# A hybrid decoder layer on one core: two score levels copied by ScalarE, the next head's work on other slots, and four weight pieces requested at once at the start

## The chip, the core and the metric

The kernel runs on 1 core of one Trainium2 chip. The metric is the device time of one execution in microseconds (us), the median of several runs. The core has five engines that run their own instruction lists in order and meet at semaphores: TensorE (PE in the profile, matmul; PEld is its weight load), VectorE (DVE), ScalarE (ACT), GpSimd (POOL) and SyncE (SP), which here only starts DMA transfers.

## What is computed

One layer of 512 tokens and 2048 channels, in float32:

```
h    = rmsnorm(x, norm_w)
proj = h @ w_in      # 2048 x 7184: gla q,k,v,gate,lowrank, hgrn q,f,i,gate
o_a  = 4 heads of chunked gated linear attention (dk 128, dv 256) on gla q, k, v, decay
o_b  = 8 heads of the same (dk 128, dv 128) on hgrn q, 1-f, i, log f
mixed = concat(head_rmsnorm(o_a) * silu(gate_a), head_rmsnorm(o_b) * silu(gate_b))
out  = rmsnorm(x + mixed @ w_out, final_norm_w)
```

Attention of a head: with b the running sum of the log decays, score(i, j) = sum over d of q_i k_j exp(b_i - b_j) for j <= i, output = scores @ v plus the decayed state of the chunks before.

## The kernel before

**Weights.** Every weight group is 2048 rows by 512 columns and comes in 8 pieces of 256 rows (512 KB). SyncE loads a piece into one of two `raw` slots; ScalarE rounds it to the high part `w_hi` (L847, helper `split`), VectorE takes the rest, `w_lo` = raw - `w_hi` (L1237), and TensorE computes three products a tile: high x high, high x low, low x high (L554). `w_hi` and `w_lo` have four slots; ScalarE and VectorE split piece p+3 at step p, and ScalarE first waits until TensorE is done with the piece whose slot it takes. A load waits until VectorE has split the piece two before it.

**Slots.** One piece gives four banks of six products. TensorE's list of a group is thus 32 slots of six products (slot 4p + c), and a table hangs the small matmuls of the attention heads behind given slots: T transposes of the decayed keys, L five score levels, U state update (needs `kdT`), O outputs (need all scores in `att` and the state), M mean square of the output (needs `sq_lo`). ScalarE and VectorE have their own tables: a list of steps behind the split of piece p, p = 0 to 7. All three lists were written by hand, and each engine runs its own strictly in order.

**Groups.** 0 and 1: values (by token tile first, in the opening). 2 and 3 (G_A): queries and keys. Then a block of products with sums of weights. G_C to G_C+3: HGRN queries and forget gates, while the four GLA heads and the first two HGRN heads run; G_E to G_E+2: gates, with two HGRN heads a group (`hg_pair`; u = 0 in slots 0 to 15, u = 1 in slots 16 to 31); G_E+3, and the output projection. GpSimd copies and adds weights in DRAM beside that, paced by TensorE's pieces.

**A head.** VectorE: `args` is the running sum of decays (a scan, L1370), `ends` three instructions on it (L1377 to L1382), `early` the decayed keys and queries (from L1392); they are done for the next head while the present one runs. `quads`, `arg(l)`, `scale(l)` prepare the operands of the score levels; `scale(5)` writes `ql` last (L1324). `scores(l)` copies a level from PSUM into `att`: levels 0 to 3 under a mask (L1335, L1348, L1354), level 4, which stands for two score levels packed in one bank, plainly (L1361 twice, L1365). `states` builds the state (L1407, L1410), `cut` the low part of the squared output (L1422), `norm` scales the output (L1428). ScalarE does the exponentials (L868), the decay (`decay`, a logarithm, L872), the evictions of outputs (`take`) and the root (`rstd`).

**Opening.** Norm weights come as one row; TensorE spreads it over the partitions with matmuls against ones (L670), VectorE copies two banks of it, ScalarE the other two (L935). ScalarE squares x tile t and sums (L939, `squares`), VectorE multiplies by the inverse root and the norm weights (L1452, `normalise(t, half)`), TensorE transposes (L681), ScalarE and VectorE cut the result into `h_hi` (L946, `highs`) and `h_lo` (L1459, `lows`). Fillers (L706) are transposes of the identity whose result nobody reads. SyncE's order: norm row, x tile 0, pieces 0 and 1, x tile 1, and then, behind a wait for the first split, piece 2, piece 3, tiles 2 and 3, the other pieces.

## Time and profile before

| | us |
|---|---|
| median of 3 runs | 877.03 (876.88 to 877.4) |
| the profiled execution | 877.31 |
| its span on the core | 875.6 |
| PE busy | 855.6 (98%) |
| DVE busy | 602.3 (69%) |
| ACT busy | 413.1 (47%) |
| POOL busy | 85.1 (10%) |

The span is first to last instruction of the profiled execution; its own time is 1.7 us longer. Busy time is the union of an engine's instructions. Matmuls are pipelined, so a row of 0.39 us may be followed by the next start after 0.227 us, and PE busy is not PE at its peak. A row of the timeline gives start, duration (with xN: from the first start to the last end), engine, line, operation, tiles written <- read, shapes, and in brackets the idle time of the engine before it with what ended it.

### The profile page before, as it was taken

All of it is one profiled execution on the core that took longest, in us unless ns stands there. A gap on an engine that the chain in (4) does not pass through costs nothing.

```text
span 875.6 us, 13716 instructions
## 1 busy us (share of the span) xinstructions
PE 855.6 (98%) x5379; PEld 698.8 (80%) x5379; DVE 602.3 (69%) x982; ACT 413.1 (47%) x554; POOL 85.1 (10%) x128
## 2 busy tenths in 40 slices
PE   8999999999999999999999999999999999999996
PEld 5886888888888878888778778778788888888885
DVE  5723377753587747577887888889885678556756
ACT  6621442324445325273464655745555455335454
POOL 4010111110000001011111100000111100000000
PEclk9999999999999999999999999999999999999999
DMA  7386569989755846567776655545776988865654
GB/s 263 96 276 217 168 186 236 202 193 242 237 173 154 276 145 202 166 181 162 165 156 149 140 176 160 164 131 181 153 159 136 289 201 268 309 203 181 202 172 192
DMA packets 75170, 167.74 MB, mean 192 GB/s; under 512 B 7333, under 2 KB 15561, under 8 KB 73961
## 3 DMA queue, kind: packets, MB, share of 16 engines
q1 hardware_dynamic: 45266, 108.02, 37.4%
q0 software_dynamic: 16896, 50.34, 26.8%
q10 hardware_dynamic: 12952, 8.61, 3.5%
q8 instruction: 38, 0.62, 0.3%
q14 instruction: 18, 0.15, 0.1%
HBM read 158.56 MB, written 58.72 MB: 248 GB/s over the span
## 4 chain that ended last, share of the span: by engine, by line
PE 72%; DVE 16%; ACT 5%; issue 3%; DMA 3%; DVEq 1%; ACTq 0%
PE main L554 42%; PE main L805 8%; PE main L747 5%; PE sc L805 4%; DMA raw<-in_w_in 3%; DVE w_lo L1237 3%; PE po L805 2%; PE st L805 2%; DVE att L1348 1%; ACT w_hi L847 1%; PE sc L612 1%; PE sc L747 1%; PE po L640 1%; PE po L643 1%; PE st L625 1%
## 5 line engine op out<-in xcount | busy, mean ns | idle before, releaser
L554 PE MATMUL main<-h_hi,w_hi 128*128 128x512 f32 x640 | 256.6, 401 | 0.1
L554 PE MATMUL main<-h_hi,w_lo 128*128 128x512 f32 x640 | 250.0, 391 | 0.0
L554 PE MATMUL main<-h_lo,w_hi 128*128 128x512 f32 x640 | 249.6, 390 | 0.0
L1237 DVE TENSOR_TENSOR w_lo<-raw,w_hi 128x1024 fp32r<-128x1024 f32 x102 | 124.6, 1222 | 118.0 <-ACT w_hi L847 117.1
L847 ACT ACTIVATE w_hi<-raw 128x1024 fp32r<-128x1024 f32 x102 | 107.8, 1058 | 192.4 <-PE main L554 134.7
L554 PEld LDWEIGHTS main<-h_hi,w_lo 128*128 128x128 f32 x640 | 120.1, 188 | 26.0
L554 PEld LDWEIGHTS main<-h_hi,w_hi 128*128 128x128 f32 x640 | 120.2, 188 | 25.6 <-issue 0.5
L554 PEld LDWEIGHTS main<-h_lo,w_hi 128*128 128x128 f32 x640 | 120.4, 188 | 23.1
L868 ACT ACTIVATE ex<-ex 128x512 f32<-128x512 f32 (+2 forms) x84 | 52.4, 641 | 59.1 <-DVE ex L1377 49.2
L554 PE MATMUL main<-w_hi,h_hi 128*128 128x512 f32 x128 | 50.5, 395 | 0.3 <-DVE val L1491 0.3
L1708 DVE TENSOR_TENSOR w_lo<-feat,w_hi 128x1024 fp32r<-128x1024 f32 x26 | 31.8, 1224 | 27.4 <-ACT w_hi L1161 27.2
L554 PE MATMUL main<-w_hi,h_lo 128*128 128x512 f32 x128 | 49.9, 390 | 0.0
L554 PE MATMUL main<-w_lo,h_hi 128*128 128x512 f32 x128 | 49.9, 390 | 0.0
L526 POOL DMA_DIRECT2D w_sum<-in_w_out x32 | 21.0, 655 | 267.0 <-PE main L554 191.7
L1161 ACT ACTIVATE w_hi<-raw 128x1024 fp32r<-128x1024 f32 x27 | 28.6, 1061 | 35.9 <-PE main L805 21.8
L1708 DVE TENSOR_TENSOR w_lo<-raw,w_hi 128x1024 fp32r<-128x1024 f32 x27 | 33.0, 1224 | 17.2 <-ACT w_hi L1161 17.1
L1161 ACT ACTIVATE w_hi<-feat 128x1024 fp32r<-128x1024 f32 x26 | 27.5, 1059 | 32.6 <-PE main L805 19.4
L534 POOL DMA_DIRECT2D w_sum<-w_sum x24 | 19.7, 820 | 126.3 <-PE main L554 111.9
L906 ACT ACTIVATE feat<-po 128x512 f32<-128x512 f32 (+1 forms) x16 | 9.5, 596 | 46.2 <-PE po L643 46.0
L805 PE MATMUL main<-w_hi,s_hi 128*128 128x512 f32 x80 | 31.1, 389 | 0.0
L805 PE MATMUL main<-w_lo,s_hi 128*128 128x512 f32 x80 | 31.1, 389 | 0.0
L805 PE MATMUL main<-w_hi,s_lo 128*128 128x512 f32 x80 | 31.1, 389 | 0.0
(307 smaller groups left out, 1494.1 us busy)
## 6 DMA issues: line engine op xcount, KB each, us to landing
raw<-in_w_in SPq DMA_DIRECT2D x104, 512.0 KB, 4.6
w_sum<-in_w_out POOLq DMA_DIRECT2D x48, 512.0 KB, 5.0
w_sum<-in_w_in POOLq DMA_DIRECT2D x24, 512.0 KB, 6.0
w_sum<-w_sum POOLq DMA_DIRECT2D x24, 512.0 KB, 5.4
raw<-w_sum SPq DMA_DIRECT2D x24, 512.0 KB, 3.5
feat<-w_sum SPq DMA_DIRECT2D x24, 512.0 KB, 3.5
raw<-in_w_out SPq DMA_DIRECT2D x14, 512.0 KB, 4.6
feat<-in_x SPq DMA_DIRECT2D x6, 1024.0 KB, 7.4
```

The costliest lines, as they stand in the source:

```text
L526: pool.dma_start(w_sum[pair, j, q], weight_piece(pair, source, q)).then_inc(w_copied[pair * len(XS) + j], 16)
L534: pool.dma_start(w_sum[pair, j, q], weight_piece(pair, source, q), accum_op=ALU.add, max_dma_last_dim=4 * PK * GW).then_inc(w_added[pair * ...
L554: mm = pe.matmul(main[c][:, :], a, b, start=(k == 0 and j == 0), stop=(k == KT - 1 and j == 2))
L612: mm = pe.matmul(into[l][b * BW:b * BW + m, to:to + w], kl[KL[l]][:, c * P + b * BW:c * P + b * BW + m], (eq4 if l in (1, 2) else queries( ...
L747: mm = pe.matmul(d_banks[bank][a][:, :], left, right, start=(q == 0 and kk == 0 and j == 0 and idx not in D_ADDS), stop=(q == QP - 1 and k ...
L805: mm = pe.matmul(banks[other or bank][a][:, cols], left, right, start=(k == 0 and j == 0 and idx not in ADDS_ON), stop=(k == KT // 2 - 1 a ...
L847: act.activation(w_hi[:, q % SPL, :, :], raw[:, q % RAW, :, :], ACT.Copy).then_inc(hi_ok, 1)
L868: act.activation(dst, src, ACT.Exp, scale=scale).then_inc(exp_ok, 1)
L906: act.activation(feat[:, q_tile + xx, :], po[:, :], ACT.Copy)
L1161: act.activation(w_hi[:, q, :, :], src, ACT.Copy).then_inc(hi_ok, 1)
L1237: dve.tensor_tensor(w_lo[:, q % SPL, :, :], raw[:, q % RAW, :, :], w_hi[:, q % SPL, :, :], ALU.subtract).then_inc(lo_ok, 1)
L1708: dve.tensor_tensor(w_lo[:, q, :, :], src, w_hi[:, q, :, :], ALU.subtract).then_inc(lo_ok, 1)
```

## The change

- `scores(4)` leaves VectorE. ScalarE gets a new step `far` with the same three copies, behind its split of the step where the outputs are still to come; `sc_ok` now counts four copies a head (NEAR), and a semaphore `far_ok` says that the plain copies are done. VectorE's `cp(3)` waits for it, and so does TensorE's level 0 of the next head.
- VectorE: `sl(5)` before `states(0)` in every head; the next head's `ends` before `cp(3)`; in the G_E groups the next head's `args` a weight piece sooner, and with it ScalarE's `decay` and load of values.
- TensorE: levels 3 and 4 of most heads one slot later, the first state update from slot 3 to 5, the mean square of u = 0 from slot 15 to 14.
- Opening: x tile 0 in two halves, squared each as it comes; pieces 2 and 3 go to a place of their own (`first_raw`) and are requested without a wait; the right half of the norm weights comes by a DMA that repeats the row over the partitions, in place of two matmul broadcasts and ScalarE's two evictions; the left half of tile 0 is normalised in two parts; seven fillers instead of four before the first transposes.
- Group 0: VectorE's split of the last step goes behind its copies of the four banks.

```
--- SyncE
-                    if not (isinstance(n, int) and n < RAW):
-                        sp.wait_ge(lo_ok, n - last + 1)
+                    if not (isinstance(n, int) and n < 2 * RAW):
+                        early = RAW if isinstance(n, int) and n < 3 * RAW else 0
+                        sp.wait_ge(lo_ok, n - last - early + 1)
+                    if isinstance(n, int) and RAW <= n < 2 * RAW:
+                        sp.dma_start(first_raw[:, s, :, :], rows.rearrange("(k p) n -> p k n", p=P)).then_inc(
+                            first_in[s], 16)
+                        continue
-            x_tile(0)
+            for a in range(2):
+                h = slice(a * D // 2, (a + 1) * D // 2)
+                sp.dma_start(xin[:, 0, h], x[0:P, h]).then_inc((x_left, x_in[0])[a], 16)
             group(w_in, C_GV, G_V, range(0, 2))
+            sp.dma_start(nwb[:, D // 2:], norm_w[D // 2:].partition_broadcast(P)).then_inc(nb_in, 16)
             x_tile(1)
--- TensorE
-                            pe.wait_ge(sc_ok, H * NL + (l - 1))
+                            pe.wait_ge(sc_ok, H * NEAR + (l - 1))
+                        elif l == 0 and not (isinstance(H, int) and H == 0):
+                            pe.wait_ge(far_ok, H * 1)
-                        pe.wait_ge(sc_ok, H * NL + NL)
+                        pe.wait_ge(sc_ok, H * NEAR + NEAR)
-            for j in range(4):
+            for j in range(2):
                 pe.matmul(main[j][:, :], ones[0:1, :], nrow[:, j * 512:(j + 1) * 512], start=True,
-            filler(4)
+            filler(7)
-            shared = dict(T=0, L=[4, 4, 4, 8, 8], U=[3, 12], O=[11, 15], M=20)
+            shared = dict(T=0, L=[4, 4, 4, 9, 9], U=[5, 12], O=[11, 15], M=20)
             second = dict(T=17, L=[18, 21, 21, 25, 25], U=[20], O=[28], M=31)
             earlier = alone | dict(U=[13, 20], O=[19, 22], M=26)
+            alone |= dict(L=[12, 12, 12, 17, 17])
-                    todo |= head_tasks(hg_at(m, u) | dict(T=z, L=[z + 4, z + 4, z + 4, z + 8, z + 8], U=[z + 3],
-                                                          O=[z + 11], M=z + 15 - u))
+                    todo |= head_tasks(hg_at(m, u) | dict(T=z, L=[z + 4, z + 4, z + 4, z + 9, z + 9], U=[z + 5],
+                                                          O=[z + 11], M=z + 14))
--- ScalarE
+                def far():
+                    act.wait_ge(sc_ps, H * NL + NL)
+                    act.wait_ge(sc_ok, H * NEAR + 3)
+                    att_at = att.rearrange("p (c n) -> p c n", c=NT)
+                    got_at = sc[0].rearrange("p (c n) -> p c n", c=NT)
+                    s = LV[PACKED]
+                    for b in range(2):
+                        act.activation(att_at[2 * b * s:(2 * b + 1) * s, :, (2 * b + 1) * s:(2 * b + 2) * s],
+                                       got_at[b * s:(b + 1) * s, :, b * s:(b + 1) * s], ACT.Copy)
+                    s = P // 2
+                    act.activation(att_at[0:s, :, s:], got_at[s:P, :, s:], ACT.Copy).then_inc(far_ok, 1)
-            squares(0)
+            act.wait_ge(x_left, 16)
+            step(act.activation(junk[:, 0:D // 2], xin[:, 0, 0:D // 2], ACT.Square, accum_out=rs[:, 4:5]))
+            step(act.activation(rs[:, 4:5], rs[:, 4:5], ACT.Identity, bias=cst[:, 2:3], scale=1.0 / D))
+            act.wait_ge(x_in[0], 16)
+            step(act.activation(junk[:, 0:D // 2], xin[:, 0, D // 2:], ACT.Square, accum_out=rs[:, 0:1]))
+            step(act.activation(rs[:, 0:1], rs[:, 0:1], ACT.Sqrt, bias=rs[:, 4:5], scale=1.0 / D))
+            act.sem_inc(xss, 1)
             split(0, -3)
-            broadcast(2)
             highs(0, [0])
-            broadcast(3)
-                        4: [g["take"](0)], 5: [g["take"](1)], 7: [g["rstd"]]}
+                        4: [g["far"], g["take"](0)], 5: [g["take"](1)], 7: [g["rstd"]]}
-                        2: [s["decay"], s["values"], s["early"], g["take"](0)],
+                        2: [s["decay"], s["values"], g["far"], s["early"], g["take"](0)],
-                    todo[z] = [h["quads"], h["keys"], lv(3)]
+                    todo[z] = [h["quads"], h["keys"], lv(3)] + [f for x in nxt for f in (x["decay"], x["values"])]
-                    todo[z + 2] = [f for x in nxt for f in (x["decay"], x["values"], x["early"])] + [h["take"](0)]
+                    todo[z + 2] = [h["far"]] + [x["early"] for x in nxt] + [h["take"](0)]
--- VectorE
+                    if l == 3:
+                        dve.wait_ge(far_ok, H + 1)
-                    else:
-                        ... the three copies of level 4
-                        2: [cp(0), cp(1), cp(2), sl(4), g["states"](0), sl(5)],
-                        3: [cp(3), cp(4)], 5: [g["states"](1), g["cut"]], 7: [g["norm"]]}
+                        2: [cp(0), cp(1), cp(2), sl(4), sl(5), g["states"](0)],
+                        3: [cp(3)], 5: [g["states"](1), g["cut"]], 7: [g["norm"]]}
-                        2: [s["args"], cp(3), cp(4), s["ends"]], 3: [g["states"](1), s["early"], g["cut"]],
+                        2: [s["args"], s["ends"], cp(3)], 3: [g["states"](1), s["early"], g["cut"]],
-                        6: [nxt["args"], cp2(3), cp2(4), nxt["ends"], nxt["early"], s["cut"]], "end": [s["norm"]]}
+                        6: [nxt["args"], nxt["ends"], cp2(3), nxt["early"], s["cut"]], "end": [s["norm"]]}
-                    todo[z] = [h["quads"], ar(4), sl(3), ar(5)]
-                    todo[z + 1] = [cp(0), cp(1), cp(2), sl(4), h["states"](0), sl(5)]
-                    todo[z + 2] = ([x["args"] for x in nxt] + [cp(3), cp(4)]
-                                   + [f for x in nxt for f in (x["ends"], x["early"])] + [h["cut"]])
+                    todo[z] = [h["quads"], ar(4), sl(3), ar(5)] + [x["args"] for x in nxt]
+                    todo[z + 1] = [cp(0), cp(1), cp(2), sl(4), sl(5), h["states"](0)]
+                    todo[z + 2] = ([x["ends"] for x in nxt] + [cp(3)] + [x["early"] for x in nxt] + [h["cut"]])
-            normalise(0, 0)
+            normalise(0, 0, slice(0, 512))
+            normalise(0, 0, slice(512, D // 2))
-            group(0, {}, values(0), 1)
+            group(0, {}, values(0), 1, NP - 1)
```

## Rows read from the trace of the kernel before

**Rows 1.** Busy time in long stretches: us, PE, PEld, DVE, ACT, POOL, PEclk, DMA, GB/s.

```profile
67.00:282.00 215.00, 215.00 (x948) 175.35 (x949) 123.95 (x157) 82.81 (x104) 20.42 (x25) 1.00 0.75 201
282.00:662.00 380.00, 371.77 (x3214) 303.45 (x3213) 301.10 (x622) 191.24 (x284) 43.05 (x55) 1.00 0.64 168
```

**Rows 2.** The chain that ended last: start, us, what.

```profile
98.53 107.48 PE main L554 x474
```

**Rows 3.** Waits of TensorE: us in total, times, longest.

```profile
PE sc L612 <- DVE ql L1324: 5.9, 5, 1.3
...
PE po L650 <- DVE sq_lo L1422: 1.7, 4, 0.7
...
PE main L554 <- DVE val L1491: 0.3, 1, 0.3
```

**Rows 4.** Timeline of TensorE, the waits one by one.

```profile
401.74 0.65 PE L612 MATMUL sc<-ql,kl 128*32 128x32 f32 x32 [0.88 <-DVE ql L1324]
...
444.05 0.50 PE L650 MATMUL po<-lrw,ones_r 128*128 128x512 f32 x1 [0.60 <-DVE sq_lo L1422]
...
501.62 0.50 PE L650 MATMUL po<-lrw,ones_r 128*128 128x512 f32 x1 [0.69 <-DVE sq_lo L1422]
...
565.02 0.93 PE L625 MATMUL st<-vst_h,kdT 128*128 128x128 f32 x6 [0.19 <-ACT kdT L901]
...
575.52 0.65 PE L612 MATMUL sc<-ql,kl 128*32 128x32 f32 x32 [1.30 <-DVE ql L1324]
```

**Rows 5.** Timeline of VectorE in one head of a G_E group.

```profile
573.75 0.28 DVE L1407 COPY state<-st 128x128 f32<-128x128 f32 x1
574.07 0.73 DVE L1410 SCALAR_TENSOR_TENSOR state<-state,dec,st 128x128 f32<-128x128 f32 x2
...
576.52 1.22 DVE L1370 TENSOR_TENSOR_SCAN bcum<-reset,gdec 128x512 f32<-128x512 uint8 x1
...
578.30 0.58 DVE L1361 COPY att<-sc 32x128 f32<-32x128 f32 x2 [0.23 <-DVE att L1354]
...
579.25 0.54 DVE L1377 TENSOR_TENSOR ex<-bcum 128x384 f32<-128x384 f32 x1
...
580.98 0.56 DVE L1392 TENSOR_TENSOR kd<-feat,ex 128x384 f32<-128x384 f32 x1 [0.17 <-DVE ex L1382]
...
585.85 0.69 DVE L1422 TENSOR_TENSOR sq_lo<-po,lrw 128x512 fp32r<-128x512 f32 x1
```

**Rows 6.** Timeline of all engines in the opening.

```profile
2.74 7.16 PE L670 MATMUL main<-val,kd 1*128 1x512 f32 x8 [2.74 <-DMA val<-in_norm_w]
...
6.05 1.91 ACT L939 ACTIVATE feat<-feat 128x2048 f32<-128x2048 f32 x1 [3.94 <-DMA feat<-in_x]
...
9.47 0.58 ACT L935 ACTIVATE feat<-main 128x512 f32<-128x512 f32 x1
...
10.74 1.92 PE L681 MATMUL sc<-ident,feat 128*128 128x128 f32 x8
...
12.47 0.69 DVE L1459 TENSOR_TENSOR h_lo<-sc,h_hi 128x512 fp32r<-128x512 f32 x1 [1.31 <-ACT h_hi L946]
...
13.62 0.48 PE L554 MATMUL main<-w_hi,h_hi 128*128 128x512 f32 x1
...
15.05 1.28 DVE L1452 SCALAR_TENSOR_TENSOR feat<-feat,rs 128x1024 f32<-128x1024 f32 x1
...
17.03 1.28 DVE L1452 SCALAR_TENSOR_TENSOR feat<-feat,rs 128x1024 f32<-128x1024 f32 x1
...
18.37 1.10 PE L681 MATMUL sc<-ident,feat 128*128 128x128 f32 x8 [0.66 <-DVE feat L1452]
```

**Rows 7.** Two microseconds of the opening, columns as in the first group.

```profile
6.00:8.00 2.00, 2.00 (x4) 0.67 (x3) 0.69 (x1) 1.95 (x2) 1.48 (x9) 1.00 1.05 407
```

**Rows 8.** The eviction of the transposed keys, ScalarE: ns min/median/max, first and last start.

```profile
L901 ACT ACTIVATE kdT<-st x12: 470/477/491, 296.6 to 648.0; 128x384 f32<-128x384 f32 x12
```

**Rows 9.** Timeline of TensorE, first outputs of the head in G_C+2.

```profile
406.54 0.60 PE L640 MATMUL po<-att,vst 128*128 128x128 f32 x4
```

More of the change, by code:

```diff
@@ L222, in hymba_kernel @@
         nrow = val[0:1, 0:2, :].rearrange("p a n -> p (a n)")
+        first_raw = val[:, 2:4, :].rearrange("p s (k n) -> p s k n", k=PK)
         ones = kd[:, 0:P]
@@ L674, in transposes @@
             def transposes(t, half):
-                pe.wait_ge(xn_ok, 2 * t + half + 1)
                 for j in (2 * half, 2 * half + 1):
+                    if t == 0 and j == 0:
+                        pe.wait_ge(xq_ok, 1)
+                    else:
+                        pe.wait_ge(xn_ok, 2 * t + half + 1)
                     if t:
@@ L1236, in split, with group @@
                 dve.wait_ge(hi_ok, first_piece(G) + (q + 1))
-                dve.tensor_tensor(w_lo[:, q % SPL, :, :], raw[:, q % RAW, :, :], w_hi[:, q % SPL, :, :],
+                first = isinstance(G, int) and RAW <= G * NP + q < 2 * RAW
+                dve.tensor_tensor(w_lo[:, q % SPL, :, :], (first_raw if first else raw)[:, q % RAW, :, :],
+                                  w_hi[:, q % SPL, :, :],
                                   ALU.subtract).then_inc(lo_ok, 1)
-            def group(G, tasks, take, first=0):
+            def group(G, tasks, take, first=0, last=NP):
                 for p in range(NP):
-                    if p >= first:
+                    if first <= p < last:
                         split(G, p)
@@ L1248, in group @@
                     take(c)
+                for p in range(last, NP):
+                    split(G, p)
                 for f in tasks.get("end", ()):
@@ L1355, in scores @@
                                             got).then_inc(sc_ok, 1)
-                    else:
-                        s = LV[PACKED]
-                        for b in range(2):
-                            to = att[2 * b * s:(2 * b + 1) * s, :].rearrange("p (c n) -> p c n", c=NT)
-                            got = sc[l % 2][b * s:(b + 1) * s, :].rearrange("p (c n) -> p c n", c=NT)
-                            dve.tensor_copy(to[:, :, (2 * b + 1) * s:(2 * b + 2) * s], got[:, :, b * s:(b + 1) * s])
-                        s = P // 2
-                        _, a = halves(att[0:s, :], s)
-                        _, got = halves(sc[l % 2][s:P, :], s)
-                        dve.tensor_copy(a, got).then_inc(sc_ok, 1)
                 def args():
+                    if not (isinstance(H, int) and H == 0):
+                        dve.wait_ge(arg_ok, H * NARG)
                     if nx == 1:
@@ L1444, in _, with normalise @@
             dve.tensor_copy(ones_r[:, :], ones).then_inc(onesr_ok, 1)
-            def normalise(t, half):
-                h = slice(half * D // 2, (half + 1) * D // 2)
-                if half == 0:
+            def normalise(t, half, cols=slice(0, D // 2)):
+                h = slice(half * D // 2 + cols.start, half * D // 2 + cols.stop)
+                if half == 0 and cols.start == 0:
                     dve.wait_ge(xss, t + 1)
```

49 lines of the change are left out of this document (28 added, 21 removed).

## The prediction

> **What bounds the kernel now.** I read the long stretches first: from 67 to 282 us TensorE has no idle time, so the change has nothing to win there. What is left is the opening and the twelve attention heads, 282 to 662 us, with TensorE busy 371.77 of 380, VectorE 301.10 and ScalarE 191.24 [rows 1]. In the chain that ended last, 474 products take 107.48 us, 0.227 each, so a slot of six is 1.36 us [rows 2].
>
> TensorE's list of waits names the places: five waits for `ql` (the query operand of level 5) with 5.9 us, four for `sq_lo` before the mean square with 1.7, one for `val` at the end of the first group with 0.3 [rows 3]. The single places stand in the timeline; to each I add 0.15 us for what is lost around it (my allowance), so 0.88 costs 1.03, 0.60 costs 0.75, 0.69 costs 0.84, and the other two of the four share what is left of the 1.7, 0.35 each. Waits for `kdT` before the state update, 0.19 idle, cost about 0.5 with both sides, at the head of each G_E group [rows 4]. The releaser is nearly always VectorE, whose list in a head runs without holes, each instruction starting 0.08 us before the one before it ends [rows 5]. So each head is a race between an in-order VectorE list and TensorE's slots; ScalarE, half idle, is not the bound.
>
> In the opening TensorE runs at the lower clock level (1.2 GHz): eight transposes from 10.74 us take 1.92 us, eight from 18.37 take 1.10. The chain is: x tile landed and squared (6.05 to 8.0), normalised, transposed from 10.74, `h_lo` at 12.47, before which VectorE idles 1.31 us, ScalarE evicting norm-weight banks (0.58 each, one at 9.47) meanwhile. The products begin at 13.6. From normalise(0,1) at 15.05 on, VectorE is nearly full, and TensorE waits for it at 18.37 [rows 6].
>
> **The change, the opening.** (a) x tile 0 in halves. From 6 to 8 us the queues move 407 GB/s [rows 7], so 0.5 MB is 1.3 us: the left half lands near 4.7, the right one near 6.0 as now. Its square, half of 1.91, and a scalar step go before 6.05; behind stand half a square (1.0), its read (0.2) and the root (0.3): the sum of squares is done at 7.7, not 8.5. (b) Two of four norm-row broadcasts leave TensorE: half of 7.16, so it is free at 6.2; seven fillers of 0.213 end at 7.7. Transposes start once 512 columns are normalised, 8.0 + 0.7 = 8.7, not 10.74. (c) Without the evictions ScalarE has the first w_hi (1.06) at 8.9, `h_hi` (0.6) at 10.5, the next w_hi at 11.5. VectorE: two normalises to 9.4, `w_lo` (1.22) to 10.6, `h_lo` (0.7) to 11.3, `w_lo` to 12.8, so normalise(0,1) at 12.8, not 15.05. Products start at 11.3, not 13.6, but what counts is what VectorE sets: normalise(1,0) at 15.1, not 17.03, if x tile 1 has landed by 12.5. (d) Has it? Ahead of it stand 1 MB of x, 1 MB of weights and the 0.5 MB norm row; with its own 1 MB that is 3.5 MB, 8.9 us at that rate from about 3.3 (6.0 less 1 MB): 12.2, plus issue. Just in time. Pieces 2 and 3 and tiles 2 and 3 follow at once and land near 14, 15, 18 and 20, ahead of use. Gain 1.9 us; bounds 0.4 (R1, R4) and 2.4. (e) The last split of the first group goes behind four value copies of 0.68: the wait for `val` goes, 0.3 + 0.15 [rows 3]; that piece is needed two pieces (10.9 us) later, so the 2.7 us of copies hide. Opening: -2.4 us, carried whole through 67 to 282 us.
>
> **The heads.** VectorE loses two 32x128 copies and one 64x256 copy a head; from the 0.23 idle before them to the next instruction at 579.25 that is 1.2 us [rows 5]. ScalarE gets them. No row has ScalarE copying such pieces; the nearest, 128x384 from PSUM, takes 477 ns [rows 8]. Narrower ones should be less: I take 0.3, 0.3 and 0.4, 1.0 a head; bounds 0.5 and 1.5. It is a wait too: `cp(3)` stands behind `far_ok`, `far` behind level 5's scores, and VectorE's next `early` and split are queued behind `cp(3)`, ScalarE's exponentials behind `far`. From the last level (slot 9) to the outputs (slot 11) lie two slots, 2.7 us: 1.0 + 0.4 for `cp(3)` fits.
> The other moves on the same list [rows 5]: levels 4 and 5 a slot later, +1.36 for `ql` to arrive. The states (0.28 + 0.73) behind `sl(5)`: `ql` 0.97 sooner. The scan ahead of it, in the G_E groups alone: 1.14 later (1.22 less overlap). `ends` ahead of `cp(3)`, 579.25 to 580.98: the outputs' operand 1.7 later, except in the first two heads. Then:
> - G_C: 1.36 + 0.97 is more than its wait (a fifth of 5.9, and 0.15): -1.3. G_C+1 has none: 0.
> - G_C+2: the 1.03 goes likewise. `cp(3)` ends 0.3 after where the packed copies ended (-1.2 - 0.3 for the move forward, + 1.7, + 0.1), at 405.8; TensorE, by 1.03 earlier than its 406.54 [rows 9], waits 0.3. The 0.75 before the mean square goes, the cut being 1.2 sooner. -0.7 - 0.75.
> - A G_E group, on the head around 575: `ql` comes 0.17 later, at 575.6. TensorE without its waits (1.30 + 0.15, and 0.5) and a slot on arrives at 574.9: waits 0.7. Then 0.6 and two slots bring it to the outputs at 579.0, while VectorE from 575.6 has states 0.97, a split 1.14, `ends` 1.65, `cp(3)` 0.4: 579.8, waits 0.8. Today the outputs start at 580.3 (575.52 + 0.6 + three slots + 0.1): -0.5. The mean square at slot 14 is reached at 585.5, the cut ends 5.5 after `cp(3)` (580.98 to 586.5 today), 585.3: hidden by 0.2. Its root done a slot sooner, the next w_hi follows slot 15 at once and the second head keeps 1 us in hand; its wait of 0.35 for `sq_lo` goes. -0.85 for the second group, -0.5 for the third, which has no such wait.
> - G_C+3 with the first G_E group: the 0.84 at 501.62 goes, but ScalarE's stores and table loads there do not wait for TensorE, so it meets the next head's exponentials instead and ends at the same 0.5 before today, plus the 0.35: -0.9.
> Sum 1.3 + 1.45 + 0.85 + 0.5 + 0.9 = 5.0, less 0.1: -4.9. The state update at slot 5 costs nothing: its reader, the states, stands a copy chain later on VectorE; without that cover it is the old 0.5 a group.
> Against the profiled run's own 877.31 (span 875.6 and 1.7 around it): 877.3 - 2.4 - 4.9 = 870.0; the median is 0.3 lower, and for margins of 0.2 I give 0.5 back: **870.2 us**.
>
> **Rivals.**
> R1, the clock. The fillers now end 1.0 before the first transposes, a hole that the present run has not. If the level stays low through the first twelve products, each costs 0.454: they end at 16.8, the next sixteen transposes and six fillers cost 2.3 more, and of the 1.9 some 1.5 is lost: 871.7. Against: VectorE's normalise(1,0) lets TensorE wait until 16.4 anyway.
> The Trainium skill (TensorE: Matmul & The Clock Gate, section "What's actually happening") says that the throttled state is the default and activity releases it, and its "Part 4: PE-mode transpose" that a transpose does not count as busy in the same way; by that this rival would be the likelier. This trace speaks against the second half: from 9.83 only transposes and fillers ran, and the products behind them ran at the higher level.
> R2, the wait moves whole. Scan and `ends` put 2.8 us in front of the outputs against 1.2 removed. If the waits come back in full, the heads give 0: 874.6. For it: in each G_E group the race is already lost by 0.7 and 0.8. Against: both are in the sum.
> R3, slower: ScalarE's copies. From 2.3 us a head on (2.7 less `cp(3)`) each us more shows at the outputs, and VectorE stands idle behind `cp(3)`. At about 3.0 the heads' gain is used up; at 3.6 (1.2 a copy) it is 1.3 in each of nine heads, less the output waits already counted, and as much again on VectorE: near 879. Against: the 128x384 row.
> R4, the loads: x tile 1 lands 1.5 us later than reckoned behind five transfers: 871.7 to 872.1.
> R5, more: VectorE's hand in the second heads grows and no output wait forms: 2 us more, 868.2.
>
> **Numbers.** Forecast 0.62 (own range 868.7 to 872.0), R1 0.08, R2 0.12, R3 0.03, R4 0.07, R5 0.08. Range 867.6 to 874.3: all but R3, most of R2 and the far end of R5. Same is within 0.2%, 1.75 us, about what this measurement can tell from no change; part of R2's spread lies there. Faster 0.90, same 0.06, slower 0.04.
>
> **What would show it.** First product near 11.3, normalise(1,0) near 15.1; no wait for `val`; ScalarE rows of 32x128 and 64x256 at 0.3 and 0.4; in each G_E group one wait of 0.7 for `ql` and one of 0.8 at the outputs, `kdT` and most of `sq_lo` gone from TensorE's list. Wrong if a ScalarE copy takes over 0.8, if VectorE idles before `cp(3)`, or a weight piece comes late.

## The result and the profile after

The changed kernel takes 872.18 us (median of 5, 871.84 to 872.32), the kernel before 877.03 (876.88 to 878.36) beside it: ratio 0.9935, 95% interval 0.9922 to 0.9948. It is faster by 4.85 us, and 2.0 slower than the forecast of 870.2. The profiled execution took 872.29 us with a span of 870.4. One of the five executions of the later kernel kd_early ran throughout at a granted clock of 0.56 and took 1425 us; it is left out of the numbers of that kernel.

The long stretches, with columns as in [rows 1]:

```profile
67.00:282.00 215.00, 215.00 (x950) 175.39 (x949) 123.76 (x156) 83.33 (x105) 20.34 (x25) 1.00 0.75 200
282.00:662.00 380.00, 375.35 (x3240) 307.43 (x3239) 289.21 (x586) 202.60 (x322) 43.76 (x56) 1.00 0.64 170
```

The first stretch is as before. In the second TensorE has 3.6 us more of busy time in the same 380, VectorE gave up 11.9 us and ScalarE took 11.4: the twelve heads' copies changed hands. TensorE's waits, in total, number and longest:

```profile
PE sc L626 <- DVE ql L1364: 2.1, 3, 0.8
...
PE po L654 <- DVE att L1396: 1.4, 4, 0.4
PE st L603 <- DVE kd L1426: 0.5, 1, 0.5
```

Against [rows 3], `ql` fell from 5.9 to 2.1 and the rows for `sq_lo` and `val` are gone, and so is the 0.4 for `kdT`. New are 1.4 at the outputs for `att`, in four places, and 0.5 at the first transposes of `kd` for VectorE; two single waits of 0.3 (for `ex`) and 0.2 (for `feat`, from ScalarE) are new too and small. The single places on TensorE, as in [rows 4]:

```profile
292.70 0.55 PE L603 MATMUL st<-ident,kd 128*128 128x128 f32 x3 [0.45 <-DVE kd L1426]
...
404.37 0.71 PE L654 MATMUL po<-att,vst 128*128 128x128 f32 x4 [0.27 <-DVE att L1396]
...
516.25 0.65 PE L626 MATMUL sc<-ql,kl 128*32 128x32 f32 x32 [0.82 <-DVE ql L1364]
...
520.30 0.68 PE L654 MATMUL po<-att,vst_h 128*128 128x128 f32 x4 [0.44 <-DVE att L1396]
...
572.14 0.65 PE L626 MATMUL sc<-ql,kl 128*32 128x32 f32 x32 [0.82 <-DVE ql L1364]
...
576.19 0.68 PE L654 MATMUL po<-att,vst_h 128*128 128x128 f32 x4 [0.43 <-DVE att L1396]
```

And the copies that ScalarE took over (ns min/median/max, first and last start):

```profile
L938 ACT ACTIVATE att<-sc x12: 380/380/383, 310.0 to 656.5; 64x256 f32<-64x256 f32 x12
...
L935 ACT ACTIVATE att<-sc x24: 266/267/269, 309.5 to 656.2; 32x128 f32<-32x128 f32 x24
```

Two small copies of 0.27 and one of 0.38 are 0.91 us a head; the forecast had 1.0.

**Where the time came from.** I set the start of the same TensorE instruction in the two traces side by side. The difference, after minus before, at the points where it changes:

| point | before us | after us | difference |
|---|---|---|---|
| first group, transposes of `ex` | 66.39 | 65.87 | -0.52 |
| first `kd` transposes | 293.06 | 292.70 | -0.36 |
| G_C, first outputs | 313.86 | 312.24 | -1.62 |
| G_C+3, first `kd` transposes | 445.99 | 443.01 | -2.98 |
| second G_E group, first `kd` transposes | 560.23 | 556.43 | -3.80 |
| third G_E group, first `kd` transposes | 616.89 | 612.34 | -4.55 |
| last head, outputs | 663.79 | 658.70 | -5.09 |

Between 66 and 293 us it first grows to -0.81 (the wait for `val` is gone), and then 0.45 of it is lost at the `kd` transposes. So in this pair of traces the opening is worth 0.36 where the heads begin, not 2.4, and the heads themselves give 4.73 against a forecast of 4.9. Such a difference holds for two executions: the changed opening also ran in four kernels of the experiments (args_back, ends_late, far_dve, lev8), which reached the transposes of `ex` between 65.34 and 65.78 and the `kd` transposes between 292.10 and 292.70, and the old opening reached `ex` at 66.11 in heads_only. Differences of some 0.5 us in the opening are therefore within what one code does by itself. The opening after, to set beside [rows 6]:

```profile
6.93 1.06 ACT L985 ACTIVATE feat<-feat 128x1024 f32<-128x1024 f32 x1
...
8.76 1.42 DVE L1486 SCALAR_TENSOR_TENSOR feat<-feat,rs 128x512 f32<-128x512 f32 x2
...
9.57 1.97 PE L698 MATMUL sc<-ident,feat 128*128 128x128 f32 x8 [1.45 <-DVE feat L1486]
...
12.90 0.78 PE L566 MATMUL main<-w_hi,h_hi 128*128 128x512 f32 x1
...
13.43 1.91 ACT L971 ACTIVATE feat<-feat 128x2048 f32<-128x2048 f32 x1 [0.67 <-DMA feat<-in_x]
13.44 1.28 DVE L1486 SCALAR_TENSOR_TENSOR feat<-feat,rs 128x1024 f32<-128x1024 f32 x1
...
15.84 0.17 DVE L1485 RECIPROCAL rs<-rs 128x1 f32<-128x1 f32 x1 [0.52 <-ACTq L973]
...
16.04 1.29 DVE L1486 SCALAR_TENSOR_TENSOR feat<-feat,rs 128x1024 f32<-128x1024 f32 x1
...
17.79 1.04 PE L698 MATMUL sc<-ident,feat 128*128 128x128 f32 x8
```

Three things stand in these rows. TensorE stood idle for 1.45 us before the first transposes, and behind that hole the products ran 0.43 apart (12.90 to 15.2), in place of 0.227: the lower level of 1.2 GHz, read from the spacing, since the granted-clock column says 1.00 throughout the opening. In the kernel before the same products ran 0.23 apart from 13.94 on, but for two gaps of 0.32 and 0.34. And x tile 1, whose square is the row at 13.43, landed at 13.4, not 12.2 to 12.5: VectorE stands 0.52 us for its root and normalise(1,0) comes at 16.04, against 17.03 before and 15.1 in the forecast. And the transposes that read its result come at 17.79 without a wait, 0.46 after it ended: in this execution TensorE, held up by its slow products, was the later of the two.

### The profile page after: what moved, and what is told of

The parts are those of the page before. It is cut to its first block, busy times and chain, and to the rows that moved or that the text cites. A ratio compares the mean times of both kernels' runs of the same rounds, so it can differ in the third digit from the quotient of the medians.

```text
span 870.4 us, 13758 instructions
## 1 busy us (share of the span) xinstructions
PE 853.6 (98%) x5378; PEld 699.7 (80%) x5378; DVE 591.0 (68%) x947; ACT 422.9 (49%) x591; POOL 85.0 (10%) x128
## 4 chain that ended last, share of the span: by engine, by line
PE 80%; DVE 10%; ACT 4%; issue 3%; DMA 1%; ACTq 0%; DVEq 0%; SPq 0%
PE main L566 50%; PE main L822 8%; PE main L763 5%; PE sc L822 4%; PE st L822 2%; PE po L822 2%; PE po L654 2%; DVE w_lo L1274 2%; PE sc L626 1%; PE sc L763 1%; PE po L657 1%; PE st L639 1%; DVE att L1390 1%; DMA raw<-in_w_in 1%; ACT w_hi L870 1%
## 5 line engine op out<-in xcount | busy, mean ns | idle before, releaser
L1274 DVE TENSOR_TENSOR w_lo<-raw,w_hi 128x1024 fp32r<-128x1024 f32 x100 | 122.1, 1222 | 121.7 <-ACT w_hi L870 121.0
L870 ACT ACTIVATE w_hi<-raw 128x1024 fp32r<-128x1024 f32 x100 | 105.7, 1058 | 194.1 <-PE main L566 140.3
L1197 ACT ACTIVATE w_hi<-raw 128x1024 fp32r<-128x1024 f32 x27 | 28.6, 1061 | 34.4 <-PE main L822 18.5
L1743 DVE TENSOR_TENSOR w_lo<-raw,w_hi 128x1024 fp32r<-128x1024 f32 x27 | 33.0, 1224 | 14.9 <-ACT w_hi L1197 14.8
```

The costliest lines, as they stand in the source:

```text
L870: act.activation(w_hi[:, q % SPL, :, :], (first_raw if first else raw)[:, q % RAW, :, :], ACT.Copy).then_inc(hi_ok, 1)
L1197: act.activation(w_hi[:, q, :, :], src, ACT.Copy).then_inc(hi_ok, 1)
L1274: dve.tensor_tensor(w_lo[:, q % SPL, :, :], (first_raw if first else raw)[:, q % RAW, :, :], w_hi[:, q % SPL, :, :], ALU.subtract).then_in ...
L1743: dve.tensor_tensor(w_lo[:, q, :, :], src, w_hi[:, q, :, :], ALU.subtract).then_inc(lo_ok, 1)
```

## The experiments

Each kernel was run beside the kernel before on the same chip, whose medians there were 877.68, 877.51 and 877.63 us in the three sets. The changed kernel was not among them; its 872.18 was measured in another set, so that a difference of 0.3 us to it means nothing by itself. The traces, one execution each, have to decide, and in the opening they scatter by some 0.5 us, as said above.

**heads_only.** The kernel before with the hunks of the heads alone: the three ScalarE copies and their two semaphores, the slots, and VectorE's and ScalarE's order. The opening and the order of copies and split in group 0 are the old ones.

> The kernel before with the attention heads of the change alone; its opening is the old one. Sum theory: opening and heads add up without meeting, since the difference of the two traces stays constant from 66 us until the first head; the heads gave 4.3 us in the changed kernel, of which one place lost 0.45 (a weight piece beside value stores that did not come earlier although TensorE did). With the old opening TensorE comes to that place 0.8 us later and the loss should not form: 877.0 - 4.3 to 4.7 = 872.3 to 872.7. Rival (the opening is worth nothing by itself, the later list takes it all back): 872.0 to 872.2, as the changed kernel.

Measured 872.89 us, ratio 0.9947 (0.9932 to 0.9962). On TensorE it is level with the kernel before at the first `kd` transposes (293.08) and 4.77 ahead at the end. That answers it: the heads are worth 4.8, and nearly all of the whole change. But the loss at `kd` was there with the old opening too. TensorE came there 0.6 earlier and waited (idle 0.60) until the same instant. The expectation that it would not form was wrong. It came earlier by two things that the edit does not explain: it reached the transposes of `ex` 0.28 sooner, and the wait for `val` was not there (next product at 66.28, not 66.89), although the order of copies and split was the old one. So that wait can be absent without the hunk that was to remove it.

**x1_first, fill13 and both.** The two explanations of the opening, one edit each:

```
-            sp.dma_start(nwb[:, D // 2:], norm_w[D // 2:].partition_broadcast(P)).then_inc(nb_in, 16)
             x_tile(1)
+            sp.dma_start(nwb[:, D // 2:], norm_w[D // 2:].partition_broadcast(P)).then_inc(nb_in, 16)
```

```
-            filler(7)
+            filler(13)
             transposes(0, 0)
```

> The changed kernel with 13 fillers in place of 7 ahead of the first transposes, so that TensorE has no idle hole from 8.1 to 9.6 us. Clock theory: the hole is why the granted clock rises only near 15.4 us here and near 13.2 before; without it the twelve first products (0.43 apart) run in part at 0.22, the transposes of x tile 1's predecessor end sooner, and the opening gains 0.3 to 0.5: 871.7 to 871.9. Load theory: normalise(1,0) waits for x tile 1, which lands at 13.4 whatever the clock, so the rise moves and the end does not: 872.0 to 872.4, normalise(1,0) still at 16.0.

> The changed kernel with x tile 1 requested before the 0.5 MB norm row instead of after it. Load theory: the tile lands about 1.3 us sooner (0.5 MB at some 390 GB/s), near 12.1 instead of 13.4; ScalarE squares it sooner, VectorE's 0.52 us of idle time ahead of its next step goes, and normalise(1,0) comes near 15.2 to 15.5 instead of 16.04: 871.3 to 871.7. Clock theory: TensorE's late transposes behind products at the lower level set the next step, so of this 0.2 at most is left: 872.0 to 872.2. A third outcome: the norm row lands at 12.2 instead of 10.9 and, if the first products needed it, makes it slower by up to 1.

> Both edits together: 13 fillers, and x tile 1 requested before the norm row. If load and clock are two waits one behind the other on the same path (VectorE idle 0.52 for the tile, then 0.55 for ScalarE, which waits for TensorE's transposes), each alone hides behind the other in part and both together give the whole: 0.9 to 1.4 us, 870.8 to 871.3. If one of them alone sets the end, this equals the better of the two single runs within 0.2.

Measured: fill13 872.01 us (ratio 0.9933, 0.9919 to 0.9946), x1_first 871.58 (0.9929, 0.9916 to 0.9943), both 871.23 (0.9926, 0.9912 to 0.9939). With 13 fillers the hole is gone, the level rises within the first eight transposes (1.42 us, between 1.92 and 1.1), fillers and products run at the higher one, and yet the trace is only 0.11 ahead of the changed kernel at 66 us:

```profile
9.51 1.42 PE L698 MATMUL sc<-ident,feat 128*128 128x128 f32 x8 [0.16 <-DVE feat L1486]
10.76 1.04 PE L723 MATMUL main<-ident 128*128 128x128 f32 x8
12.00 0.47 PE L566 MATMUL main<-w_hi,h_hi 128*128 128x512 f32 x1 [0.20 <-DVE h_lo L1494]
12.31 0.40 PE L566 MATMUL main<-w_lo,h_hi 128*128 128x512 f32 x1
```

Eight fillers take 1.04 us here (1.92 in the changed kernel), so the rise fell among transposes and fillers, with no product before it. The first product comes at 12.00 instead of 12.90, and TensorE then waits for VectorE, which waits for x tile 1. But that tile came later in this execution than in the changed kernel's: its square starts at 13.97 instead of 13.43 and normalise(1,0) at 16.58 instead of 16.04, so that the gain of the clock was covered by a later load, which the edit does not touch. With the tile requested first, ScalarE squares it at 12.62:

```profile
12.14 0.59 ACT L978 ACTIVATE h_hi<-sc 128x512 fp32r<-128x512 f32 x1
12.62 1.91 ACT L971 ACTIVATE feat<-feat 128x2048 f32<-128x2048 f32 x1
```

There normalise(1,0) starts at 15.50, and TensorE is 1.08 us ahead of the changed kernel at 66 us; both edits give 1.17. But x1_first changed more than the load: with the same seven fillers and the same hole (1.48) its level rose at 13.35, not at 15.2. The trace of lev8, whose opening is that of the changed kernel, tells the two apart. Its level was up at the first product, tile 1 came as in the changed kernel (square at 13.55, normalise(1,0) at 16.16), and TensorE waited for it:

```profile
17.50 1.09 PE L698 MATMUL sc<-ident,feat 128*128 128x128 f32 x8 [0.85 <-DVE feat L1485]
```

lev8 is at `ex` at 65.34, 0.53 ahead of the changed kernel with the same loads, and 0.55 behind x1_first with an early rise as well. So in the changed kernel's trace the late rise and the late tile cost about a half of the 1.08 each. They are two limits on one step: where the tile is as late as 13.97 the clock costs nothing (fill13, 65.76, against args_back with its tile at 13.98, 65.78), and where the clock is late an earlier tile gains little (x0_whole, whose square starts at 13.05: the transposes at 17.31 without a wait, 0.37 after normalise(1,0) ended, and `ex` at 65.40). The four kernels with both edits (x1_fill13, kd_early, late_m15, late_m15_args1) lie at 64.58 to 64.81, all below the 65.34 to 65.87 of the five with the changed opening. With both, VectorE waits 0.35 for the norm row, which now lands behind the tile, and normalise(1,0) is at 15.54:

```profile
13.54 1.29 DVE L1486 SCALAR_TENSOR_TENSOR feat<-feat,rs 128x1024 f32<-128x1024 f32 x1 [0.35 <-DMA feat<-in_norm_w]
```

**x0_whole.** x tile 0 in one transfer and one square, in the changed kernel:

```
-            for a in range(2):
-                h = slice(a * D // 2, (a + 1) * D // 2)
-                sp.dma_start(xin[:, 0, h], x[0:P, h]).then_inc((x_left, x_in[0])[a], 16)
+            x_tile(0)
...
-            act.wait_ge(x_left, 16)
...
+            squares(0)
```

> The changed kernel with x tile 0 requested and squared whole, as in the kernel before. In the changed kernel the halves landed at 5.34 and 6.62 us where the whole tile had landed at 5.96, and the sum of squares was ready at 8.41 against 8.38 before. Theory A (the halves pay with a later landing what they win by squaring early): the whole tile lands near 6.0, the sum is ready near 8.4, and the time is the same within 0.2: 872.0 to 872.4. Theory B (the right half is late because four more requests follow at once and share the queues, not because of the halves): the whole tile lands near 6.6 too, the sum is ready at 9.1, and the opening loses 0.4 to 0.7: 872.6 to 872.9.

Measured 872.14 us (0.9937, 0.9924 to 0.9951). The whole tile is landed and its square starts at 6.02, and VectorE's first normalise starts at 8.70, against 8.76 in the changed kernel. Theory A holds: the halves buy nothing. In the changed kernel ScalarE works without a pause from 5.42 on, half square, read, scalar step, half square, read and root, and what the early start wins is spent on the extra read and step. Tile 1 was squared at 13.05 here, ahead of the 13.43 to 13.98 of the six traces with halves and the old load order; one trace does not show that the halves cost it.

**kd_early.** On top of both opening edits (x1_fill13), VectorE does `early` of head 0 before the third split of its group:

```
             step(dve.memset(att[:, :], 0.0))
+            gla_head(0)["early"]()
...
-                todo = {0: [g["args"], g["ends"]] * (h > 0) + [g["early"]], 1: [g["quads"], ar(4), sl(3), ar(5)],
+                todo = {0: [g["args"], g["ends"], g["early"]] * (h > 0), 1: [g["quads"], ar(4), sl(3), ar(5)],
```

> The kernel with 13 fillers and x tile 1 requested first (871.2), and in it VectorE's first key-decay product of head 0 (and what belongs to it) ahead of the third split of the group instead of behind it. There TensorE stood 0.64 us over its own pace at 291.56, at the transposes of `kd`; VectorE's split waits for a weight piece that lands 6 to 7 us after its request, and `kd` is queued behind that split although its own operands have been ready for 5 us. In-order theory: the wait goes and nothing is behind it: -0.5 to -0.65, 870.6 to 870.8, and TensorE's later instructions come earlier by that. Rival (the piece itself is what TensorE needs next): its products of that piece then wait instead, and the time is the same, 871.1 to 871.3.

Measured 870.2 us (median of four; with the fifth it is the 870.4 that an expectation below names), ratio 0.9917 (0.9902 to 0.9933). VectorE's timeline in the changed kernel:

```profile
285.47 0.48 DVE L1639 MEMSET att<- 128x512 f32 x1
290.95 1.23 DVE L1274 TENSOR_TENSOR w_lo<-raw,w_hi 128x1024 fp32r<-128x1024 f32 x1 [4.99 <-ACT w_hi L870]
292.10 0.55 DVE L1426 TENSOR_TENSOR kd<-feat,ex 128x384 f32<-128x384 f32 x1
```

and in this one:

```profile
284.19 0.48 DVE L1639 MEMSET att<- 128x512 f32 x1
284.71 0.56 DVE L1426 TENSOR_TENSOR kd<-feat,ex 128x384 f32<-128x384 f32 x1
...
289.69 2.55 DVE L1274 TENSOR_TENSOR w_lo<-raw,w_hi 128x1024 fp32r<-128x1024 f32 x2
```

In the changed kernel `kd` stands behind a split that waits 5 us for a weight piece. Taken ahead of it, `kd` is done 7 us sooner, TensorE no longer waits there, and the first scores come 0.81 before those of the kernel with both opening edits (298.06 against 298.87). Of this 0.12 was there at 66 us already, so the move is worth about 0.7, at the upper end of the 0.5 to 0.65 expected.

**far_dve.** VectorE makes the three plain copies again, just ahead of `cp(3)`; slots and order are the changed ones.

```
-                        4: [g["far"], g["take"](0)], 5: [g["take"](1)], 7: [g["rstd"]]}
+                        4: [g["take"](0)], 5: [g["take"](1)], 7: [g["rstd"]]}
...
+                        dve.wait_ge(sc_ps, H * NL + NL)
...
+                            dve.tensor_copy(att_at[2 * b * w:(2 * b + 1) * w, :, (2 * b + 1) * w:(2 * b + 2) * w],
+                                            got_at[b * w:(b + 1) * w, :, b * w:(b + 1) * w])
+                        dve.tensor_copy(att_at[0:P // 2, :, P // 2:], got_at[P // 2:P, :, P // 2:]).then_inc(far_ok, 1)
```

> The changed kernel with the three plain copies of levels 4 and 5 done by VectorE again, just ahead of `cp(3)`, at the changed slots. Theory: it is the copies' 1.2 us a head on VectorE that decides the race in each head; TensorE then waits about 1.0 more at each of the outputs and VectorE has no slack to win it back: about +8 by counting (0.9 a head over nine heads), 878 to 880, slower than the kernel before. Rival (slots matter, not who copies): ScalarE's turn and its two semaphores cost about what the copies do, and the moves of slots made the gain: 872 to 874.

Measured 879.36 us (1.0021, 1.0012 to 1.0031): slower than the kernel before, and 7.2 above the changed one (7.4 at the last outputs in the traces). TensorE's waits from 285 to 665 us:

```profile
PE po L654 <- DVE att L1391: 8.0, 7, 1.6
PE sc L626 <- DVE ql L1351: 2.3, 3, 0.9
```

The waits at the outputs are 8.0 in place of 1.4, and `ql` is as it was. The loss of 0.6 to 1.3 us falls in seven of the twelve heads; the first two (G_C, G_C+1) and the second heads of the three G_E groups lose nothing, so VectorE's time behind level 5 decides seven races and not all. The slot moves without the move of the copies are worth less than nothing.

**lev8.** Levels 4 and 5 a slot earlier again, in all heads where the change moved them:

```
-            shared = dict(T=0, L=[4, 4, 4, 9, 9], U=[5, 12], O=[11, 15], M=20)
+            shared = dict(T=0, L=[4, 4, 4, 8, 8], U=[5, 12], O=[11, 15], M=20)
...
-            alone |= dict(L=[12, 12, 12, 17, 17])
...
-                    todo |= head_tasks(hg_at(m, u) | dict(T=z, L=[z + 4, z + 4, z + 4, z + 9, z + 9], U=[z + 5],
+                    todo |= head_tasks(hg_at(m, u) | dict(T=z, L=[z + 4, z + 4, z + 4, z + 8, z + 8], U=[z + 5],
```

> The changed kernel with levels 4 and 5 put back one slot earlier (slot 8 instead of 9 in the heads that share a group and in the G_E groups, 16 instead of 17 in G_C). In-order theory: TensorE now meets the level-5 wait for `ql` a slot (1.36 us) earlier; in G_C that wait was 1.26 and was gone after the change, in the three G_E groups it is 0.97, 0.97, 0.66 now and would be 2.3, 2.3, 2.0. But a wait taken at slot 8 leaves the outputs at slot 11 with three slots behind it instead of two, and there TensorE waits 0.6, 0.6, 0.46 now: those go. Per G_E group some +1.36 - 0.6, in G_C up to 0.3, in G_C+2 0.4: +1.5 to +2.5, 873.7 to 874.7. Rival (the list on VectorE alone sets the pace of each head, wherever TensorE takes the wait): within 0.4 of the changed kernel, 871.8 to 872.6.

Measured 877.89 us (1.0001, 0.9986 to 1.0015), 3.2 above the top of what I expected: the whole gain of the change is gone. The ten executions spread from 877.11 to 879.38; the trace is that of the fastest, and it is 4.95 us behind the changed kernel's at the end of the heads. The waits are those foreseen, 2.34, 2.31 and 2.00 us over TensorE's own pace, and in the first G_E group the outputs come 0.75 later, as counted. In the second and third they come 2.2 and 2.4 later still. The windows show why (columns as in [rows 1]; the last but two is the granted clock):

```profile
516.00:520.00 4.00, 4.00 (x47) 3.33 (x48) 3.90 (x9) 2.39 (x6) 0.00 (x0) 1.00 0.24 64
572.00:576.00 4.00, 3.45 (x38) 2.80 (x39) 3.89 (x10) 1.85 (x5) 0.00 (x0) 0.57 0.32 95
630.00:634.00 4.00, 3.76 (x39) 3.01 (x40) 3.89 (x9) 2.03 (x6) 0.00 (x0) 0.57 0.77 123
```

```profile
572.55 1.08 PE L626 MATMUL sc<-ql,kl 128*32 128x32 f32 x32 [2.17 <-DVE ql L1363]
573.57 0.80 PE L566 MATMUL main<-h_hi,w_hi 128*128 128x512 f32 x1
574.16 0.63 PE L566 MATMUL main<-h_lo,w_hi 128*128 128x512 f32 x1
574.59 0.63 PE L566 MATMUL main<-h_hi,w_lo 128*128 128x512 f32 x1
```

The rows are TensorE's timeline behind the wait of the second group. After 2.17 us of standing still TensorE's level fell to 1.2 GHz: products 0.43 apart instead of 0.227, until 575.9; beyond the longer waits each of the two groups lost 1.5 us to this. It fell in two of the three groups; in the first the wait was as long and the clock stayed. Without these 3.0 us the loss is 1.95, inside the 1.5 to 2.5 of the theory.

**args_back.** The next head's scan, decay and values back in their old place in the G_E groups:

```
-                    todo[z] = [h["quads"], ar(4), sl(3), ar(5)] + [x["args"] for x in nxt]
+                    todo[z] = [h["quads"], ar(4), sl(3), ar(5)]
...
-                    todo[z + 2] = ([x["ends"] for x in nxt] + [cp(3)] + [x["early"] for x in nxt] + [h["cut"]])
+                    todo[z + 2] = ([f for x in nxt for f in (x["args"], x["ends"])] + [cp(3)] + [x["early"] for x in nxt] + [h["cut"]])
```

ScalarE's decay and values move back with them (not shown).

> The changed kernel with the next head's scan (VectorE) and decay and values (ScalarE) back in their old place in the G_E groups, two weight pieces later than now. In-order theory: `ql` comes 1.14 sooner in the first head of each group, so its waits (0.97, 0.97, 0.66) go; but the scan then stands with `ends` in front of `cp(3)`, 1.14 more there, on top of output waits of 0.60, 0.59, 0.46: they become some 1.4 to 1.7 less what TensorE, coming sooner, adds. Sum near 0 to +0.8: 872.2 to 873.0. Rival (the earlier scan is what gains, by giving the exponentials and the next head a lead): +2 or more, 874 or above. Other side: if ScalarE's decay (1.6 us) ahead of its level exponentials was what made `ql` late, -1: 871.2.

Measured 872.21 us (0.9933, 0.9916 to 0.9951), as the changed kernel. The waits moved whole: none for `ql` is left, and the outputs have them all.

```profile
PE po L654 <- DVE att L1396: 3.7, 4, 1.3
```

**ends_late.** `ends` of the next head behind `cp(3)`; the lists of G_C+2 and G_C+3 change likewise (not shown):

```
-                    todo[z + 2] = ([x["ends"] for x in nxt] + [cp(3)] + [x["early"] for x in nxt] + [h["cut"]])
+                    todo[z + 2] = ([cp(3)] + [f for x in nxt for f in (x["ends"], x["early"])] + [h["cut"]])
```

> The changed kernel with VectorE's `ends` of the next head put back behind `cp(3)` (in G_C+2, G_C+3 and the G_E groups); everything else stays. Theory of the in-order list: the output waits that are new in the changed kernel (0.43, 0.60, 0.59, 0.46 over a product pair's own time at 404.4, 520.3, 576.2, 631.6 us) are `ends` (1.65 us) standing in front of `cp(3)`; without it they go: 0.4 + 0.6 + 0.6 + 0.5, some 2.0 in all, less what the later `ends` costs the next head: 870.2 (own range 869.8 to 870.8). Rival (the wait moves on): the next head's scan and exponentials start 1.7 later, so the second heads meet the wait at `ql` or at the mean square and the gain is 0.5 or less: 871.7 to 872.3.

Measured 871.36 us (0.9928, 0.9915 to 0.9942); in the trace 0.39 is gained, the rival's size (the medians are 0.8 apart, over two sets). The waits at the outputs are all gone, but in the G_E groups TensorE now loses about 0.3 before the mean square of five of the six heads, since the `cut` stands behind `ends` and `early` as before and TensorE comes sooner.

**late_m15 and late_m15_args1.** From kd_early on: first `ends` late and the first head's mean square at slot 15, then also the scan between its two places:

```
-                                                          O=[z + 11], M=z + 14))
+                                                          O=[z + 11], M=z + 15 - u))
```

```
-                    todo[z] = [h["quads"], ar(4), sl(3), ar(5)] + [x["args"] for x in nxt]
-                    todo[z + 1] = [cp(0), cp(1), cp(2), sl(4), sl(5), h["states"](0)]
+                    todo[z] = [h["quads"], ar(4), sl(3), ar(5)]
+                    todo[z + 1] = [cp(0), cp(1), cp(2), sl(4), sl(5), h["states"](0)] + [x["args"] for x in nxt]
```

> The 870.4 kernel (13 fillers, x tile 1 first, key decay early), with `ends` behind `cp(3)` and the first head's mean square of each G_E group back at slot 15. With `ends` late alone the output waits went (0.60, 0.59, 0.46) and five waits of 0.27 to 0.37 for `sq_lo` before the mean square came in their place, and a part was lost at the start of the next group: net 0.4 in the trace. Theory: a slot more before the mean square hides the wait in the first head of each group (three of the five), 0.3 each, and with the 0.4 of before this gives 869.0 to 869.6. Rival (the root then comes a slot later, the next weight piece's split and the second head's chain are queued behind it on ScalarE and VectorE): nothing or a loss, 870.0 to 871.0.

> The kernel before this one, with the next head's scan, decay and values one weight piece later than in the change and one earlier than before it: behind the levels' operands and the state instead of ahead of them. Theory: `ql` of the first head is no longer behind the scan (1.22 less overlap), so the waits of 0.97, 0.97 and 0.66 go, and the scan falls into the time in which `cp(3)` has to wait for ScalarE's copies anyway (VectorE idles up to 2.2 us there in the second heads): -1.5 to -2.5 against the kernel before this one, 866.9 to 868.0. Rival (the scan's 1.2 us show at the outputs instead): 868.9 to 869.6, the same as without it.

(In the second edit ScalarE's decay and values move with the scan.) Measured 868.77 us (0.9893, 0.9879 to 0.9907) and 866.25 (0.9866, 0.9849 to 0.9882), both better than the ranges expected, and the second is the fastest of all: 11.4 us under the kernel before, 5.9 under the changed one. All that TensorE still waits for from 285 to 665 us is

```profile
PE sc L626 <- DVE ex L1328: 0.3, 1, 0.3
PE po L664 <- DVE sq_lo L1456: 0.3, 2, 0.2
PE main L566 <- ACT feat L1043: 0.2, 1, 0.2
```

Behind the states and ahead of the next split, the scan no longer stands in front of `ql`, and with `ends` late the outputs do not wait for it either. In the traces the second edit is worth 2.6 us over the first at the last outputs, and the first 1.2 over kd_early.

## Why the prediction was right in direction and 2 us off

Sign, place and nearly the whole size of the heads were right; the term that was mis-sized is the opening, forecast at -2.4 and worth -0.36 where the heads begin. It went in two steps: 1.6 of it was missing once the `val` wait was past (0.81 instead of 2.4), through a late tile and a late rise of the clock, and 0.45 was lost at `kd`, so that "carried whole" was wrong as well. The 872.18 lies just above the forecast's own range (868.7 to 872.0) and beside the times given for R1 (871.7) and R4 (871.7 to 872.1); both were at work, each at a part of its price. Step by step:

- **(a) x tile 0 in halves**, sum of squares at 7.7: wrong. The halves were squared from 5.42 and 6.93, not 4.7 and 6.0, and the sum was ready at 8.4, as before. x0_whole shows the halving worth nothing.
- **(b) transposes at 8.7**: 9.57, by (a). The hole that rival R1 spoke of was there, and the first products behind it ran 0.43 apart, though not all twelve. Set beside lev8 this cost 0.53 of R1's 1.5. The argument against R1, that VectorE is later anyway, holds for fill13 with its later tile and fails for the changed kernel's own trace, where the second transposes did not wait. Its page's rule (Trainium skill, "TensorE: Matmul & The Clock Gate", "Part 4: PE-mode transpose") does not describe these traces: in fill13 the level rose within the transposes from 9.51 on, and in lev8 before the first product at 12.78, and from 6.4 us on TensorE had run only transposes and fillers.
- **(c) products at 11.3**, normalise(0,1) at 12.8: 12.90 and 13.44. In fill13, where the fillers ran at the higher level, they are 12.00 and 13.25, so 0.9 and 0.2 of the delay belong to the clock; the transposes came 0.9 late by (a).
- **(d) x tile 1 landed by 12.2 to 12.5**: 13.4, rival R4 in mechanism. I had reckoned with 407 GB/s from one window [rows 7]; from 4 to 8 us the changed kernel moved 348 and then 334, and over 4 to 12 us 387. The number of open requests alone does not explain it: x0_whole, with all requests but one, moved 403 from 6 to 8 us. At 387 my own sum would have ended near 12.7, so the rate explains less than half; what held the tile until 13.4 stays open. Against x1_first the late tile cost 0.55, and together with the clock 1.1; the kernel with both edits has 1.7 over the kernel before at `ex`, of the 1.9 forecast.
- **(e) the wait for `val`**: gone, 0.29 instead of 0.45, and used up at `kd`. That the hunk removed it is not shown, since it is absent in heads_only too.
- **"Carried whole"**: right as far as 282 us, where I stopped looking. In the chain through the next 11 us no TensorE work stands in the kernel before either; it goes through VectorE, one weight load, ScalarE's w_hi, VectorE's w_lo and `kd`:

```profile
283.58 6.54 DMA raw<-in_w_in
290.15 1.07 ACT w_hi L847
...
292.45 0.55 DVE kd L1392
```

TensorE stood 0.17 over its own pace there already, so it had nothing in hand. The changed kernel asked for that piece 0.81 sooner and it took 6.99:

```profile
282.77 6.99 DMA raw<-in_w_in
```

In heads_only it took 7.14 and in the kernel with both opening edits 7.02; over all kernels with the changed heads and `kd` in its place it is 6.92 to 7.54. Why it is 0.4 to 1.0 longer in all of these I did not try; value stores run beside it, but no run took them away.
- **G_C -1.3, G_C+2 -1.45, G_C+3 with the first G_E group -0.9, second -0.85, third -0.5**: -1.26, -1.36, -0.82, -0.75, -0.54.
- **Waits of 0.7 for `ql` and 0.8 at the outputs in each G_E group**: 0.96 and 0.60 over TensorE's own pace in the first two, 0.66 and 0.46 in the third. The sum of 1.5 is right in the first two (1.1 in the third), the split is not, and in args_back, where the outputs have it all, the time is the same.
- **The state update at slot 5, `sq_lo`**: gone from the list of waits, as said.
- **R2 and R5** were refuted: a wait remained, but smaller than the one removed. **R3**: the copies take 0.91 a head, and far_dve shows what the same copies cost on VectorE, 7.2 us.

## What to carry to other kernels

Before a gain is carried to the end, follow the chain past the stretch that is full: the first place where it leaves the full engine says how much of the gain can arrive. When several transfers are brought forward together, a landing time from one window's rate is an estimate that can be 1 us off; put the one that the next step waits for ahead of the one that can be late. Before a difference between two traces is given to an edit, look at how far traces of the same code differ, and whether the clock or a load moved with it. And in an in-order list ask of each instruction not only who waits for it but who waits behind it: moving `kd` in front of a split that waits for a load, and the scan to a place where nobody waits, gave more here (0.7 and 2.6 us) than the opening's rebuilding (0.36).

## What the runs showed that I had not expected

- A long wait has a second price. In lev8, waits of 2.0 to 2.3 us dropped TensorE's granted clock to 0.57 over the next 4 us in two cases of three and cost 1.5 us more each, 3.0 of the 4.95 by which its trace is behind the changed kernel's. Waits of 0.96 never did, nor did the one of 2.02 before the second transposes of fill13 (1.09 us for eight, the higher level).
- Where the clock rises in the opening differs between executions of the same code: in the changed kernel, args_back, ends_late, far_dve and lev8, whose openings are the same, the twelve first products began at 12.8 to 12.9 us and were followed by transposes at 16.91, 16.78, 16.49, 16.04 and 15.62. With a tile as early as 13.4 to 13.5 this moved `ex` from 65.34 (lev8) over 65.44 (ends_late) to 65.87 (the changed kernel). The landing of x tile 1 differed too, from 13.4 to 14.0.
- ScalarE copies of 32x128 and 64x256 from PSUM take 267 and 380 ns, against 477 for 128x384 [rows 8].
